# The down projection's seven products: right sums made by transfers, deeper rings, activations in cells, remainders on two engines

## What is computed

```python
def conv_ffn(h, w_gate, w_up, conv_w, conv_b, w_down):
    g = causal_dwconv(h @ w_gate, conv_w, conv_b)
    return (jax.nn.gelu(g) * (h @ w_up)) @ w_down      # (1024, 2816) @ (2816, 1024)

x = x + conv_ffn(h, w_gate[i], w_up[i], conv_w[i], conv_b[i], w_down[i])
```

## Time and profile before

| | us |
|---|---|
| median of 3 runs | 3208.42 |
| lowest and highest run | 3206.19, 3209.51 |
| the profiled execution, its own time | 3210.71 |
| its span, first to last instruction | 3208.9 |
| PE busy | 3033.6 (95%) |
| DVE busy | 2311.0 (72%) |
| ACT busy | 1444.7 (45%) |
| POOL busy | 1484.2 (46%) |
| layer 0's down pass, first matmul to last | 281.3 |
| layer 1's down pass | 277.0 |

### The profile page before, as it was taken

How to read it: one execution, slowest core, us unless ns; L and a number is a source line. 1 busy time by engine, 2 the same in 40 slices (tenths; PEclk the granted TensorE clock), 3 DMA queues, 4 the chain that set the end, 5 groups by cost and what they waited for, 6 DMA issues and landing times. The chain is left out here.

```text
span 3208.9 us, 44141 instructions
## 1 busy us (share of the span) xinstructions
PE 3033.6 (95%) x14830; PEld 2513.7 (78%) x14830; DVE 2311.0 (72%) x3455; ACT 1444.7 (45%) x3125; POOL 1484.2 (46%) x951
## 2 busy tenths in 40 slices
PE   7999999999989999788899999999989999978989
PEld 6778888888868888666688887899768888856767
DVE  5699997896388888588943331999368878759972
ACT  4485438786343333233432221888343333333441
POOL 3114544573165665344622544776135556534540
PEclk9999999999999999899999999999999999989999
...
DMA packets 286198, 337.53 MB, mean 105 GB/s; under 512 B 87836, under 2 KB 180812, under 8 KB 286028
## 3 DMA queue, kind: packets, MB, share of 16 engines
...
## 5 line engine op out<-in xcount | busy, mean ns | idle before, releaser
L2154 DVE TENSOR_SCALAR_CACHE_REDUCE k_x<-k_x,l0in_cand,l0in_want 128x384 bf16<-128x384 f32 (+1 forms) x186 | 174.9, 1003 | 1.2 <-DVE l0in_before L2149 0.2
L2577 POOL TENSOR_TENSOR l0ff_w_lo<-l0ff_raw_g,l0ff_w_hi 128x512 fp32r<-128x512 f32 x64 | 93.3, 1462 | 140.2 <-ACT l0ff_w_hi L2444 140.0
L2577 POOL TENSOR_TENSOR l1ff_w_lo<-l1ff_raw_g,l1ff_w_hi 128x512 fp32r<-128x512 f32 x64 | 93.1, 1457 | 140.1 <-ACT l1ff_w_hi L2444 140.0
L78 PE MATMUL l1in_acc<-k_w_lo,k_hi 128*128 128x512 f32 x384 | 150.9, 393 | 2.4 <-PEq L99 2.4
L2473 ACT ACTIVATE k_x<-k_x 128x512 f32<-128x512 f32 x88 | 55.6, 631 | 215.9 <-DVE k_x L2671 215.9
L80 PE MATMUL l1in_acc<-k_w_hi,k_hi 128*128 128x512 f32 x384 | 150.4, 392 | 0.0
L79 PE MATMUL l1in_acc<-k_w_hi,k_lo 128*128 128x512 f32 x384 | 150.1, 391 | 0.0
L2498 ACT ACTIVATE l0ff_d_hi<-l0ff_d_raw 128x512 fp32r<-128x512 f32 x77 | 48.6, 631 | 158.7 <-DVE l0ff_d_raw L2713 135.2
L721 DVE TENSOR_TENSOR l1in_sq<-l1in_out 128x512 f32<-128x512 f32 x32 | 38.4, 1201 | 108.0 <-ACT l1in_out L658 108.0
L2498 ACT ACTIVATE l1ff_d_hi<-l1ff_d_raw 128x512 fp32r<-128x512 f32 x77 | 48.5, 630 | 147.0 <-DVE l1ff_d_raw L2713 127.5
L78 PE MATMUL l0ff_bank_g<-l0ff_d_lo,l0ff_s_hi 128*128 128x512 f32 x176 | 76.2, 433 | 33.0 <-POOL l0ff_s_lo L2581 22.5
...
## 6 DMA issues: line engine op xcount, KB each, us to landing
l0ff_d_raw<-in_w_down SPq DMA_DIRECT2D x132, 256.0 KB, 3.1
l1ff_d_raw<-in_w_down SPq DMA_DIRECT2D x132, 256.0 KB, 3.1
...
```

The source lines that it names most:

```text
L78: pe.matmul(out, a_hi, b_lo, start=start, stop=False)
L2154: tick(dve.tensor_scalar(hits[:, cols], score[:, cols], cand[:, i:i + 1].bitcast(F32), want[:, i:i + 1], ALU.is_ge, ALU.add, accum_out=exc ...
L2577: pool.tensor_tensor(buf.ring_lo[q % R][:], operand(q), buf.ring_hi[q % R][:].bitcast(F32), ALU.subtract).then_inc(w_lo_done[0], 1)
```

## The change

- The right operands that are sums, (1,0)+(1,1), (0,0)+(1,1) and (0,0)+(0,1), are no longer added on DVE. A DRAM tensor `right_sums` of 3 x 1408 x 512 is made for each layer by POOL's queue in the projection stage: six copies of 704 rows, then six transfers of 704 rows that add to it. The down pass loads one cell of it. Differences are still made on DVE.
- Products 0 and 1 change places: the first now has a left sum, (0,0)+(0,1), and a single right quarter.
- Rings are four deep (`DEEP`), and the queues prepare step z + 3 (`AHEAD`).
- The left quarters are 33 cells with places of their own, loaded one by one, from the beginning of the last gate/up group on; token tiles, later cells and the next stage's weights are spread over the products.
- From step 6 on, POOL takes the left remainders of even steps and DVE those of odd steps, with a semaphore for each.
- DVE makes one add per slot, in slots 1 to 8.
- ACT, POOL: one chunk of the next stage's weights in slot 4 of each of products 2 to 6; squares and roots in slots 0 to 3 of product 6. DVE scales in slots 2 and 4 of it.

```diff
@@ layer 1, projection_stage, POOL
             for s in range(1, S):
                 for c in range(CH):
                     low(CH * s + c)
+                    if s in (1, 2) and c < right_sums.count // 2:
+                        right_sums.copy(pool, (s - 1) * (right_sums.count // 2) + c)
+                    if s in (3, 4) and c < right_sums.count // 2:
+                        right_sums.add(pool, (s - 3) * (right_sums.count // 2) + c)
@@ layer 0, project_select_stage, POOL
                     if t % 2 == 0 and (not isinstance(s, int) or s + 1 < S):
                         low(s + 1, 1 - b, t // 2)
+                    if s == 1 and t < right_sums.count:
+                        right_sums.copy(pool, t)
+                    if s == 3 and t < right_sums.count:
+                        right_sums.add(pool, t)
@@
 DOWN = (
+    Down(((0, 0), (0, 1), ALU.add), ((1, 1), None, None), ((0, 1, ALU.add), (0, 0, ALU.subtract))),
     Down(((0, 0), None, None), ((0, 1), (1, 1), ALU.subtract), ((0, 1, ALU.add), (1, 1, ALU.add))),
-    Down(((0, 0), (0, 1), ALU.add), ((1, 1), None, None), ((0, 1, ALU.add), (0, 0, ALU.subtract))),
...
+class RightSums:
+    PIECES = 2
...
+    def copy(self, pool, i):
+        n, at = self.place(i)
+        one = DOWN[self.products[n]].right[0]
+        pool.dma_start(self.sums[n, at], self.blocks[one][at]).then_inc(self.copied, 16)
+
+    def add(self, pool, i):
+        n, at = self.place(i)
+        two = DOWN[self.products[n]].right[1]
+        pool.wait_ge(self.copied, 16 * self.count)
+        pool.dma_start(self.sums[n, at], self.blocks[two][at], accum_op=ALU.add).then_inc(self.summed, 16)
...
@@ ffn_stage, SP
             def load_down(z):
                 r, k = divmod(z, KB2)
-                if z >= 3:
-                    sp.wait_ge(d_lo_done, z - 2)
...
+                if z >= DEEP:
+                    sp.wait_ge(d_lo_done, z - DEEP + 1)
+                right_sums.load(sp, r, k, d_raw[z % DEEP], d_in[z % DEEP])
...
+                if grp == NG - 1 and n == 0:
+                    for b in range(2):
+                        sp.wait_ge(stored[b], 16 * 2 * (NG - 1) - 16)
+                    load_part(a11, (0, 0), range(2), a11_in)
+                if grp == NG - 1 and n == 3:
+                    sp.wait_ge(filled, W * grp + 2)
+                    load_part(a11, (0, 0), range(2, 7), a11_in)
+                if grp == NG - 1 and n == 6:
+                    sp.wait_ge(filled, W * grp + 4)
+                    for b in range(2):
+                        sp.wait_ge(stored[b], 16 * 2 * (NG - 1))
+                    load_part(a12, (0, 1), range(6), a12_in[0])
+                    sp.wait_ge(right_sums.summed, 16 * right_sums.count)
+                    for z in range(DEEP):
                         load_down(z)
+                if grp == NG - 1 and n == 8:
+                    sp.wait_ge(filled, W * grp + 6)
+                    load_part(a11, (0, 0), range(7, 8), a11_in)
+                    load_part(a12, (0, 1), range(6, 8), a12_in[0])
+                    load_part(a22, (1, 1), range(4), a22_in)
+            sp.wait_ge(filled, Q - 2)
+            load_part(a11, (0, 0), range(8, 11), a11_in)
+            load_part(a12, (0, 1), range(8, 9), a12_in[1])
+            sp.wait_ge(stored[0], 16 * 2 * NG)
+            load_part(a12, (0, 1), range(9, 11), a12_in[2])
+            sp.wait_ge(filled, Q)
+            load_part(a22, (1, 1), range(4, 8), a22_in)
+            sp.wait_ge(stored[1], 16 * 2 * NG)
+            for z in range(DEEP + 3, Z):
                 r, k = divmod(z, KB2)
                 load_down(z)
+                if (r, k) in ((0, 7), (0, 9)):
+                    t = k - 7
+                    for u in (t, t + 1):
+                        sp.dma_start(x[:, u, :], buf.kept[u * P:(u + 1) * P, :]).then_inc(x_in[0], 16)
...
@@ ffn_stage, POOL
             for z in range(Z):
                 r, k = divmod(z, KB2)
-                if z + 2 < Z:
-                    low_left(z + 2)
-                if r == 5 and 5 <= k < 5 + nxt.ROOTS:
-                    nfeed.root(pool, k - 5)
-                if r == 6 and k in (1, 3, 5, 7, 9):
-                    n = k // 2
+                if z + AHEAD < Z and not by_vector(z + AHEAD):
+                    low_left(z + AHEAD)
+                if r == 6 and k < nxt.ROOTS:
+                    nfeed.root(pool, k)
+                if 2 <= r <= 6 and k == 4:
+                    n = r - 2
                     pool.wait_ge(n_hi_ready, n + 1)
@@ ffn_stage, DVE
             def down_slot(z):
                 r, k = divmod(z, KB2)
-                if z + 2 < Z:
-                    sum_right(z + 2)
-                    sum_left(z + 2)
-                if r and 1 <= k <= 4:
-                    for n in (2 * k - 2, 2 * k - 1):
-                        if n < ADDS[r - 1]:
-                            add(r - 1, n)
-                if z + 2 < Z:
-                    low_right(z + 2)
-                if (r, k) == (5, 10):
-                    nfeed.scale(dve, 0)
-                if (r, k) == (6, 2):
-                    nfeed.scale(dve, 1)
+                if z + AHEAD < Z:
+                    sum_right(z + AHEAD)
+                    sum_left(z + AHEAD)
+                if r and 1 <= k <= ADDS[r - 1]:
+                    add(r - 1, k - 1)
+                if z + AHEAD < Z:
+                    low_right(z + AHEAD)
+                    if by_vector(z + AHEAD):
+                        low_left(z + AHEAD)
+                if r == 6 and k in (2, 4):
+                    nfeed.scale(dve, k // 2 - 1)
```

265 lines of the change are left out of this document (138 added, 127 removed).

## The result

| | before | after |
|---|---|---|
| median, us (runs on the same chip) | 3208.97 (4 runs, 3206.19 to 3209.93) | 3156.44 (4 runs, 3153.99 to 3161.22) |
| profiled execution, us | 3210.7 | 3161.2 |
| ratio | | 0.9836, 95% interval 0.9823 to 0.9848 |

The change is worth 52.5 us, not the 116 of the forecast, and 3156 us lies above the range.

The account below looks back on a forecast made before the run. PE, busy 95%, loses 139.5 us in the down passes to loads and DVE; 118.3 us saved there less 2 us added elsewhere gives 3094.4 us profiled, 3092 us median; range 3070 to 3135.

Parts of the forecast that it names:

- The middle: Products 1 to 5 of a down pass: 149.6 us at PE's pace plus 2 us of delay, 151.6 us.
- Rival C: Down pass: DVE still sets the pace, 11 us a pass lost in place of 2; 3110 us, chance 20%.
- preparing three steps ahead: Middle of the down pass: a step's remainders can be some 3.5 us late before PE feels it.
- For the shared DMA engines ... I take 2 us in all: Both layers' projections: the added transfers' issues stay hidden on POOL; sharing the DMA engines costs 2 us in total.
- POOL's time between two lows: Projections: POOL has room for six issues up to 4.7 us each in layer 0, 3 us in layer 1.
- T: Projections: the time one transfer's issue holds POOL, taken as 2 us and hidden.
- Rivals A and B: Projections: POOL held by issuing transfers; 12 us each gives 3240 us (chance 5%), 6 us each gives 3116 us (12%).
- The 3.1 us for a transfer beside a DVE copy: Layer 0's projection: the skill's figure, taken as an issue of 3.1 us; the sum would be 0.3 us smaller.
- Product 0: a stall of 3 us: Start of each down pass: loads for steps 7 and 8 come late on SP's queue; 3 us, bounds 0 and 10.
- rival D: Start of each down pass stays bound by transfers: 10 us of stall instead of 3; 3106 us, chance 12%.
- Product 6: a new wait of 2.2 us: Last product of each pass: PE's first turn waits 2.2 us after step 6 for product 5's eighth add; 35.5 us total.

Follow-up runs that it names:

- rings of three: The changed kernel with rings three deep and operands prepared two steps ahead, all else kept: ratio 0.9832 to the kernel before (changed kernel 0.9836).

## Why the prediction was wrong

| term | predicted, us | measured, layers 0 and 1 |
|---|---|---|
| product 0 | 32.9 | 40.65, 40.12 |
| products 1 to 5 | 151.6 | 151.0, 149.6 |
| product 6 | 35.5 | 42.61, 41.65 |
| pass | 220.0 | 234.2, 231.4 |
| lost elsewhere, both layers | 2 | 43.2 |

**The middle** was right: operands on time, DVE 27.5 to 29.9 us busy, clock 1.00. Rival C didn't come. The reason given for part of it, preparing three steps ahead, was not needed (rings of three).

**"For the shared DMA engines ... I take 2 us in all" is the step that failed**, 41 of the 67 us between 3094.4 and 3161.2. 38 of the 43.2 us are in the two projections, 33.4 and 4.6. The price of one transfer was worked out (a copy is 3.7 us of the engines) and then not multiplied, though each layer has twelve; and it was too low. 3.7 us is 1.44 MB at 393 GB/s, but the 24 transfers took 4.9% of the 16 engines' 3159 us, 6.4 us each. The changed kernel's page has that row (packets, MB, share):

```profile
q0 software_dynamic: 13056, 34.60, 4.9%
```

The overlap was wrong too. The rows that counted were ACT's waits for `l0h_raw`: 48.7 us in 12 of 16 chunks in the kernel before. ACT already stood waiting for three of four chunks, so what lands later holds its queue longer, and with it the copies out of PSUM that PE needs. The list of who waited for `l0h_raw` in the kernel before (us, times) has them, and the prediction doesn't use it:

```profile
  ACT l0in_w_hi L2017: 30.0, 6
...
  ACT l0h_w_hi L2017: 18.7, 6
```

What I weighed instead, POOL's time between two lows, asks about the engine that issues. There T was near enough: 0.7 to 1.2 us for my 2. Rivals A and B gave the strips of over 45 us that were measured (59.7, 51.5 and 51), but for POOL's reason; no rival had them for the loads' reason. The 3.1 us for a transfer beside a DVE copy that the Trainium skill gives ("SBUF — State Buffer", A bandwidth-pool intuition that's wrong (but worth ruling out)) isn't seen either. The prediction took this figure, which is for a whole transfer, for the issue, and the work of DVE here is comparisons (L2162), not copies: two issues in a row took 1.4 to 1.6 us, with DVE busy for 42.27 of the 43 us from 263 to 306. Another rule bears on it: by the Trainium skill each DMA engine takes packets in turn from the queues it has work for ("DMA: Bandwidth & Descriptors", Queues, rings and completion order). By that rule, as an estimate, a load beside a transfer would have half the engines' time, 8.8 us for 4.4; the seven late chunks took 7.7 to 13.5 us, in that direction and mostly more.

In layer 1 the same twelve transfers cost 4.6 us in this profile, between 0.1 and 4.8 us in the twelve experiments with the transfers there (268.5 to 273.2 us for 268.4 before), and at most 0.1 us in the two without them. There too the chunks are late, and there too ACT waited for most of them before. ACT's wait and the landing times for layer 1's chunks, before:

```profile
  ACT k_w_hi L646: 68.8, 15
...
DMA to landing us min/median/max: 3.6/3.9/4.9
```

and after:

```profile
  ACT k_w_hi L646: 113.2, 17
...
DMA to landing us min/median/max: 3.5/5.3/12.5
```

So a load that somebody waits for is not yet a loss; it has to reach PE. Both projections load and round a chunk in the same tile slot and fill four PSUM banks in turn. That layer 1's transfers are issued singly isn't the reason: issued singly in layer 0 they cost 50.5 us. What else differs in the rows is ACT, busy for 59 of 271 us in layer 1 and for 113 of 256 in layer 0 (before), where it also squares each tile; it may catch up in layer 1, but no run tests that. Nor is it settled what makes the loss 0.1 us in one run and 4.8 in another.

**"Product 0: a stall of 3 us"** had the right place and cause for most of it, and the wrong size: 10.7 and 10.2 us. The last store came 13.1 us after the pass began, not 9.8. From its issue to ACT's start on the cell it took 12.2 us (5.3 until the cell is issued, 6.9 until ACT has it), not the 9.4 of the prediction: that is 6.1 us later in all. The engines moved 327 GB/s from 1370 to 1380 us, not 393. The 2.3 us of steps 3 and 4 (1.6 in layer 1) had no term. I had rival D (10 us) at 12%; its bound was called half of 26.6 us, which is 13.3.

**"Product 6: a new wait of 2.2 us"** again had the place right: PE does wait for the eighth add. It took DVE's slots for on time and added only the last link. DVE had 31.7 us of work in that window by my own count, and stood behind by two slots when the turn came: PE waited 8.5 and 8.1 us. The term was priced as a total over the product, where the deadline is after step 6. One scaling of 1024 elements beside POOL's wide remainder took 3.44 us instead of 1.27.
